# A two-layer hybrid trunk on one core: attention on full 128-row tiles with its transpositions three items behind the scores, the retention output split in parts, and a key projection among the Fourier products

## The reference, cut to what matters

```python
rq, rk, rv, rg, nq, nk, nv, fu, gt = split(h @ w_in)              # for latent and context tokens
y_ret = ((groupnorm(retention(rq, rk, rv)) * gw + gb) * silu(rg)) @ ret_w_out
# neighbourhood attention: 8 heads of 64, 4 rows x 64 columns of latent tokens, 16 columns each, all context keys
s = concat([q @ k_window.T * 64**-0.5 + bias, q @ k_ctx.T * 64**-0.5])
y_na  = (softmax(s) @ v) @ na_w_out
y_fou = fft2(fu).real @ fou_w_out
y = (sigmoid(g_ret) * y_ret + sigmoid(g_na) * y_na + sigmoid(g_fou) * y_fou) @ w_o
```

## Time and profile before

| what | value |
|---|---|
| median of 3 runs | 2544.29 us (2541.22 to 2547.0) |
| profiled execution's own time | 2541.49 us |
| its span, first to last instruction | 2539.7 us |
| mean granted TensorE clock, as a share of full | 0.978 |
| PE busy | 2432.4 us (96% of the span) |
| PE weight loads | 2106.9 us (83%) |
| DVE busy | 1592.9 us (63%) |
| ACT busy | 941.9 us (37%) |
| POOL busy | 131.1 us (5%) |
| DMA | 400.62 MB, mean 158 GB/s |

### The profile page before, as it was taken

One profiled execution on the slowest core, in us unless ns is written; L12 is line 12 of the kernel. 1 busy time (PEld: TensorE's weight loads), 2 busy tenths in 40 slices (PEclk: granted clock), 3 DMA queues, 4 the chain that ended last, 5 costly groups with the idle time before them and its releaser, 6 DMA issues.

```text
span 2539.7 us, 33647 instructions
## 1 busy us (share of the span) xinstructions
PE 2432.4 (96%) x13554; PEld 2106.9 (83%) x13554; DVE 1592.9 (63%) x2098; ACT 941.9 (37%) x1373; POOL 131.1 (5%) x163
## 2 busy tenths in 40 slices
PE   6999999999999999979999999999999998996998
PEld 6988988988876788868889888889888885995996
DVE  5566658755555455486666686666786644665655
ACT  2522345433124322344224554224454213443343
POOL 2000001001000000020000010000020001001000
PEclk8999999999999999989999999999999998997999
DMA  8545665551312334445456565456565232674763
GB/s 269 154 162 167 192 194 177 169 182 34 107 41 70 125 121 136 136 144 168 159 173 192 181 209 167 153 178 192 181 183 177 92 116 81 200 244 136 229 200 124
DMA packets 476815, 400.62 MB, mean 158 GB/s; under 512 B 36341, under 2 KB 428789, under 8 KB 476405
## 3 DMA queue, kind: packets, MB, share of 16 engines
q1 hardware_dynamic: 464992, 391.18, 49.3%
q10 hardware_dynamic: 11668, 7.30, 1.0%
HBM read 397.25 MB, written 1.17 MB: 157 GB/s over the span
## 4 chain that ended last, share of the span: by engine, by line
PE 87%; DVE 7%; ACT 2%; issue 2%; DMA 1%; SPq 0%; POOL 0%; POOLq 0%; ACTq 0%; DVEq 0%
PE ps L1315 26%; PE ps L1317 25%; PE ps L1316 25%; DVE wl L835 2%; PE ps L1579 2%; PE ps L1570 1%; PE ps L1591 1%; PE ps L1513 1%; ACT wh L504 1%; PE ps L1340 1%; ACT tB L522 1%; DVE st L893 1%; PE ps L1672 1%; PE ps L1347 1%; PE ps L1371 1%
## 5 line engine op out<-in xcount | busy, mean ns | idle before, releaser
L835 DVE TENSOR_TENSOR wl<-raw,wh 128x1024 fp32r<-128x1024 f32 x576 | 701.0, 1221 | 665.3 <-ACT wh L504 663.9
L504 ACT ACTIVATE wh<-raw 128x1024 fp32r<-128x1024 f32 x576 | 609.7, 1059 | 1278.8 <-PE ps L1317 1246.3
L1315 PE MATMUL ps<-hh,wh 128*128 128x256 f32 (+1 forms) x2736 | 895.1, 327 | 32.0 <-DVE hl L926 19.8
L1316 PE MATMUL ps<-hl,wh 128*128 128x256 f32 (+1 forms) x2736 | 887.5, 324 | 0.0
L1317 PE MATMUL ps<-hh,wl 128*128 128x256 f32 (+1 forms) x2736 | 887.4, 324 | 0.0
L1315 PEld LDWEIGHTS ps<-hh,wh 128*128 128x128 f32 x2736 | 523.8, 191 | 77.7 <-DVE hl L926 20.9
L1316 PEld LDWEIGHTS ps<-hl,wh 128*128 128x128 f32 x2736 | 523.8, 191 | 41.5 <-issue 1.0
L1317 PEld LDWEIGHTS ps<-hh,wl 128*128 128x128 f32 x2736 | 523.5, 191 | 40.9
L850 DVE SCALAR_TENSOR_TENSOR acc<-araw,c,acc 128x1024 f32<-128x1024 f32 x210 | 258.3, 1278 | 41.1 <-DMA araw<-in_ada_w 39.6
L1315 PE MATMUL ps<-wh,stage_h_f 128*128 128x512 f32 x616 | 240.7, 391 | 2.0 <-DVE stage_l_f L979 2.0
L1316 PE MATMUL ps<-wl,stage_h_f 128*128 128x512 f32 x616 | 239.8, 389 | 0.0
(11 more groups left out here) (158 smaller groups left out, 2360.5 us busy)
## 6 DMA issues: line engine op xcount, KB each, us to landing
raw<-in_ffa_w SPq DMA_DIRECT2D x204, 512.0 KB, 4.0
raw<-in_ffb_w SPq DMA_DIRECT2D x168, 512.0 KB, 3.8
raw<-in_mix_w_in SPq DMA_DIRECT2D x148, 512.0 KB, 4.1
araw<-in_ada_w SPq DMA_DIRECT2D x136, 512.0 KB, 5.1
raw<-in_mix_w_o SPq DMA_DIRECT2D x24, 512.0 KB, 4.3
raw<-in_ret_w_out SPq DMA_DIRECT2D x16, 512.0 KB, 4.5
raw<-in_na_fou_w_out SPq DMA_DIRECT2D x16, 512.0 KB, 3.8
raw<-in_ada_w SPq DMA_DIRECT2D x8, 512.0 KB, 5.4
```

The lines of the kernel that those rows point to most:

```text
L504: A.activation(wh[:, s, :], raw[:, s, :], ACT.Copy).then_inc(w_rounded, 1)
L835: V.tensor_tensor(wl[:, s, :], raw[:, s, :], f(wh[:, s, :]), ALU.subtract).then_inc(w_split, 1)
L1315: T.matmul(out, a[0], b[0], start=start, stop=False)
L1316: T.matmul(out, a[0], b[1], start=False, stop=False)
```

## The change

Scores and values use the whole array. Queries go to `nq`, a slot of 128 partitions for each head in which the other head's 64 rows are zero; values go to `nv` with 128 columns for each head, of which the other head's 64 are zero. POOL writes the zeros ahead of attention. ACT, no longer DVE, copies the queries out of PSUM, in two or four pieces a unit, and copies each tile of values in two pieces. Both heads of a pair add up in one bank. Items are ordered (pair, stream, block, head of the pair), so in layer 0 four items of 512 keys and four of 256 alternate.

DVE no longer builds `jd`; it multiplies `prob` by the reciprocal in place (512 or 256 columns). PE's `turned` is a plain `T.transpose` against `ident`, and the flip is in the order in which ACT's copy writes `probT`. `prob` has four buffers, and the rounds are scores(t), turned(t-3), values(t-4).

The bias has four buffers; ACT's queue issues the loads of four heads, SP's those of the other four, earlier than before. The first gate unit of `merge` goes to bank 7 and stands in PE's list right after turned of round len(items). Retention's output is rounded in three parts and its rest taken in three: the first four of eight 128-feature blocks in round len(items), the others four rounds on, after the last values; PE waits for each part at the row that needs it. The first key unit of `na_in` stands after f_one(1) of the Fourier products, and retention's second score product waits for two tiles only.

```diff
-        in0 = [0, RET[0] + 12]
+        in0 = [0, RET[0] + 8]
-        n_items = [[(h, s, q) for h in range(NH) for s in ... for q in range(LT)]
+        n_items = [[(2 * pr + a, s, q) for pr in range(NH // 2) for s in ... for q in range(LT) for a in range(2)]
+        def q_slot(h):
+            return 4 * (h % 2) + h // 2
 # SP
-                for h in range(2, NH):
-                    sp.wait_ge(n_max, n0[l] + len(n_items[l]) // NH * (h - 1))
+                for h in range(4, NH):
+                    sp.wait_ge(n_max, n0[l] + len(n_items[l]) // 4 * (h // 2 - 2) + 3 + h % 2)
                     load_bias(sp, l, h)
 # ACT
-                        if t >= 3:
-                            act.wait_ge(n_turn, b + t - 2)
+                        if t >= 4:
+                            act.wait_ge(n_turn, b + t - 3)
...
-                    if 2 <= t < len(items) + 2:
-                        v = t - 2
+                    if 3 <= t < len(items) + 3:
+                        v = t - 3
...
-                        A.copy(probT[:, v % 2, 0:n], ps[:, 2 + v % 2, 0:n]).then_inc(n_turnc, 1)
+                        o, y = (a.rearrange("p (a c) -> p a c", c=GRID_W) for a in (probT[...], ps[...]))
+                        A.copy(o[:, :, ::-1] if items[v][1] == 0 else o, y).then_inc(n_turnc, 1)
+                    if t == len(items):
+                        act.wait_ge(n_score, b + len(items))
+                        A.copy(oh[:, 0:4, 0:N], rgz[:, 0:4, 0:N]).then_inc(o_hi, 1)
+                    if t == len(items) + 4:
+                        act.wait_ge(n_out, b + len(items))
+                        for p in (4, 6):
+                            A.copy(oh[:, p:p + 2, 0:N], rgz[:, p:p + 2, 0:N]).then_inc(o_hi, 1)
...
-                for h in range(2):
+                for h in range(4):
                     load_bias(act, l, h)
                 for j in range(8):
                     rounded(u + 4 + j)
+                    if j >= 4:
+                        act.wait_ge(unit_done, u + j + 1)
+                        ... A.activation(nq ..., ACT.Copy, scale=DH ** -0.5), two pieces, four where N > SEQ
 # DVE
-                    V.tensor_scalar(jd[:, t % 3], flip[:] if items[t][1] == 0 else ident[:], nmax[:, t % 3, 3:4], None,
-                                    ALU.mult).then_inc(n_jd, 1)
+                    w = prob[:, t % 4, 0:key_n(items[t])]
+                    V.tensor_scalar(w, w, nmax[:, t % 3, 3:4], None, ALU.mult).then_inc(n_norm, 1)
+                def low(p, n):
+                    dve.wait_ge(o_hi, 3 * l + max(p // 2, 1))
+                    V.tensor_tensor(ol[:, p:p + n, 0:N], rgz[:, p:p + n, 0:N], f(oh[:, p:p + n, 0:N]), ALU.subtract).then_inc(o_lo, 1)
+                    if t == len(items):
+                        low(0, 4)
+                    if t == len(items) + 4:
+                        dve.wait_ge(n_out, b + len(items))
+                        low(4, 2)
+                        low(6, 2)
 # PE
-                pe.wait_ge(rv_copied, NT * (l + 1))
-                scores(1)
+                pe.wait_ge(rv_copied, NT * l + 2)
+                scores(1)
+                pe.wait_ge(rv_copied, NT * (l + 1))
...
-                        ins = T.matmul(ps[:, 2 + t % 2, w], prob[:, t % 3, w], jd[:, t % 3], start=True, stop=True)
+                        ins = T.transpose(ps[:, 2 + t % 2, w], prob[:, t % 4, w], ident[:])
...
-                for t in range(len(items) + 3):
+                pe.wait_ge(nq_zero, 2 * l + 2)
+                pe.wait_ge(nv_zero, l + 1)
+                for t in range(len(items) + 4):
                     if t < len(items):
                         scores(t)
-                    if 2 <= t < len(items) + 2:
-                        turned(t - 2)
-                    if t >= 3:
-                        values(t - 3)
+                    if 3 <= t < len(items) + 3:
+                        turned(t - 3)
+                    if t == len(items):
+                        form_a(AT["merge", l], 7, (hh, hl), mid(l))
+                    if t >= 4:
+                        values(t - 4)
...
+                    if t == 1:
+                        pe.wait_ge(in_copied, c0 + 3 + RET[l] + 1)
+                        form_a(AT["na_in", l], 0, src, TOK)
...
-                    if mm == 0:
-                        pe.wait_ge(o_lo, 2 * (l + 1))
-                    form_a(v + 1, 1, (oh, ol), N)
+                    form_a(v + 1, 1, (oh, ol), N, src_at={0: (o_lo, 3 * l + 1), 4: (o_lo, 3 * l + 2), 6: (o_lo, 3 * l + 3)} if mm == 0 else {})
```

More of the change, by code:

```diff
@@ L205, in trunk @@
             fl = sb("fl", [P, FG, TOK], F32R, scope=mix)
+            with Scope() as s:
+                nq = sb("nq", [P, NH, TOK], scope=s)
             ah = sb("ah", [P, FG, TOK], F32R, scope=mix)
@@ L626, in attention @@
                 per = len(items) // NH
-                for t in range(len(items) + 4):
+                for t in range(len(items) + 5):
                     if t < len(items):
@@ L804, in _ @@
                     G.tensor_tensor(rve[:, t % 4], rve[:, t % 4], nhalf, ALU.pow).then_inc(r_rstd, 1)
+                pool.wait_ge(r_fin, r0[l] + len(r_items[l]))
+                for a in range(2):
+                    p0 = DH - DH * a
+                    G.memset(nq[p0:p0 + DH, 4 * a:4 * a + 4, 0:mid(l)], 0.0).then_inc(nq_zero, 1)
+                pool.wait_ge(nq_zero, 2 * l + 2)
+                pool.wait_ge(f_two, f0[l] + len(f_items[l]))
+                for a in range(2):
+                    ins = G.memset(nv[:, :, a::2, DH - DH * a:P - DH * a], 0.0)
+                ins.then_inc(nv_zero, 1)
                 for h in range(NH):
-                    pool.wait_ge(bias_in[h % 2], 16 * ROWS * (l * NH // 2 + h // 2 + 1))
-                    b = bias[:, h % 2].rearrange("p q (r c) -> p (q r) c", c=GRID_W)
+                    pool.wait_ge(bias_in[h % 4], 16 * ROWS * (l * NH // 4 + h // 4 + 1))
+                    b = bias[:, h % 4].rearrange("p q (r c) -> p (q r) c", c=GRID_W)
                     G.tensor_tensor(b, b, wmask[:].unsqueeze(1).broadcast_to([P, LT * ROWS, GRID_W]), ALU.add)\
@@ L1135, in maximum @@
                             dve.wait_ge(bias_masked, NH * l + h + 1)
-                        link(V.tensor_tensor(y[:, 0:SEQ], y[:, 0:SEQ], bias[:, h % 2, q], ALU.add))
+                        link(V.tensor_tensor(y[:, 0:SEQ], y[:, 0:SEQ], bias[:, h % 4, q], ALU.add))
                     link(V.tensor_reduce(nmax[:, t % 3, 0:1], y[:, 0:key_n(items[t])], AXX, ALU.max))
                     V.tensor_scalar(nmax[:, t % 3, 1:2], nmax[:, t % 3, 0:1], -1.0, None, ALU.mult).then_inc(n_max, 1)
-                for t in range(len(items) + 4):
+                def low(p, n):
+                    dve.wait_ge(o_hi, 3 * l + max(p // 2, 1))
+                    V.tensor_tensor(ol[:, p:p + n, 0:N], rgz[:, p:p + n, 0:N], f(oh[:, p:p + n, 0:N]), ALU.subtract).then_inc(o_lo, 1)
+                for t in range(len(items) + 5):
                     if t < len(items):
@@ L1320, in ready, with form_a @@
                 pe.wait_ge(w_split, u + 1)
-            def form_a(u, bank, src, n, kts=KD, row=0, last=True, n0=0):
+            def form_a(u, bank, src, n, kts=KD, row=0, last=True, n0=0, src_at={}):
                 s = u % RING
@@ L1736, in constants @@
     k = {"k_ident": np.eye(P, dtype=f32)}
-    flip = np.zeros((P, P), f32)
-    for r in range(P // GRID_W):
-        for c in range(GRID_W):
-            flip[r * GRID_W + GRID_W - 1 - c, r * GRID_W + c] = 1
-    k["k_flip"] = flip
     swap = np.zeros((P, P), f32)
```

97 lines of the change are left out of this document (46 added, 51 removed).

## The result

The changed kernel takes 2504.88 us, the median of four runs (2501.32 to 2511.34), where the kernel before took 2544.39 (2541.22 to 2547.0): a ratio of 0.985 (95% interval 0.9829 to 0.9872), 39.5 us less. The forecast was 2502. The profiled run took 2506.22 with a span of 2504.3, 35.3 less than the profiled run before.

What follows compares the result with a forecast made beforehand. PE bounds the kernel (87% of the chain), in attention a ring of waits would; savings of 24.0 + 17.5 + 3.6 less 1, 1, 0.2 and 1 make 41.9 us, taking 2541.5 to 2499.6, with 2.8 for the median 2502; range 2490 to 2519.

Steps and rivals of the forecast that it cites:

- The sum: Whole kernel: attention 24.0 + 17.5, Fourier 3.6, less 1, 1, 0.2 and 1, saves 41.9 us.
- the stretches behind them: Stages after attention: give nothing back, since merge and wo are filled by PE alone.
- Full tiles and transpositions: PE's 512-key attention item: scores 0.85, four transpositions 0.44, values 0.87, together 2.16 us instead of 3.16.
- DVE's product: Attention, DVE's 512-column product in place: 0.48 us, between 0.37 and 0.69.
- The ring: Attention: waits from scores through exponential, ACT's copy and values to later scores set 2.31 us per 512-key item, 1.30 per 256-key.
- Stages: Attention's first product to first oh product: 76.5 us in layer 0, 55.0 in layer 1, saving 24.0 and 17.5.
- The 2.5 us charged in layer 0 for a half clock: Start of layer 0's attention: a 5 us stretch at half clock, costing 2.5 us (0 to 6).
- Late rounds: Attention's last rounds: exponentials stay 3.81 us apart in layer 0 and 4.75 in layer 1.
- Fourier: Fourier loop, both layers: the key unit fills PE's waits of 1.94 and 1.67 us, saving 3.6, at least 2.5.
- Retention: Retention's earlier second score product: saves nothing; if the clock halves, some 1 us lost (0 to 3, both layers).
- Bias loads: ACT's 16 bias DMAs, 10.6 us, ahead of rounding unit 4 of na_in: cost 1 us (0 to 3) in layer 1.
- Rival C: Attention: the clock stays at half throughout, PE's 512-key item takes 4.3 us, kernel 2565 us, slower than before; chance 6%.

Runs made afterwards that it cites:

- copy_first: Changed kernel with ACT's copy of item t-3's transposed tile put ahead of the exponential of item t: 2487.2 us.
- bias_spread: Changed kernel with ACT's 16 bias loads issued four at a time behind the first four weight roundings instead of all ahead of them: 2500.2 us.
- key_back: Changed kernel with the first key unit put back behind the Fourier products: 2505.8 us.
- ret_back: Changed kernel with retention's second score product waiting again for all four copies of the values: 2505.7 us.
- half_tiles: Changed kernel with scores back on 64-row tiles and values on 64-column tiles, transpositions and order kept: 2520.8 us.
- scores_half: Changed kernel with only the scores back on 64-row tiles, values on full tiles: 2521.0 us.

## Why the prediction was right, point by point

The sum was 41.9 for a measured 35.3 (profiled) or 39.5 (medians); its terms were right in kind, and their errors have both signs, so the total is better than its parts: the attention stages saved 45.0 for a forecast 41.5, and the stretches behind them, put at nothing, took 6.9 more in the profiled run.

- **Full tiles and transpositions, 0.85, 0.44, 0.87 and 2.16 an item.** Measured 0.86, 0.44, 0.89 and 2.19, undisturbed only with the copy first. The prediction credited the transpositions with 0.65; 0.45 is theirs and 0.2 the switch's. DVE's product, estimated at 0.48, took 0.487.
- **The ring.** Right, by copy_first. 2.31 an item was forecast; in layer 1 at full clock scores stood 2.19 to 2.56 apart with one step of 3.27, 2.46 in the mean. In layer 0 long and short items can't be told apart as they were priced, since a round holds the scores of one item and the values of the fourth before it: steps are 1.53 to 2.56 in either kind. A head pair, four items of each kind, took 15.98 (762.12 to 778.10) for a forecast of 4 x 2.31 + 4 x 1.30 + 1.2 = 15.6; the sum is right, the division into 2.31 and 1.30 is not shown.
- **Stages.** 76.5 and 55.0 forecast, 75.3 and 52.75 measured. The 2.5 us charged in layer 0 for a half clock did not come, though PE waited 1.88 there; in layer 1 the clock was half for some 3.2 us at the start and as long in the last rounds (0.87 of 12.4 us, 0.93 of 23.3). That layer 0 was spared is luck of this execution: with the same attention code it took 75.3 in bias_spread, but 77.0 in key_back and 78.7 in ret_back, at clocks of 1.00, 0.96 and 0.93.
- **Late rounds** unchanged at 3.81 and 4.75: right.
- **Fourier, 3.6.** 2.2 to 2.4 in layer 0 and 2.1 in layer 1 where it stands, a little more than forecast. No wait stands before the first `f_two`. In layer 1 the bias loads took it back and more: the stretch from Fourier to attention grew by 1.6.
- **Retention, nothing, 1 for the clock.** The loss was 1.8 in the profiled run; ten other profiled runs with the same order don't have it.
- **Bias loads, 1 (0 to 3).** Mis-sized: 3.7 in the profile (72.4 to 68.7) and 4.7 by bias_spread's median. I saw the 10.6 us on ACT's queue but set them against DVE's pace behind the burst, not against the backlog: the first split came 11.2 us late, and DVE had too little slack to make it up before PE's value units.
- **Rival C, the half clock (6%).** It did not come, but the reason given against it, that the full clock had held through half-used tiles in the earlier trace rows, was weak. half_tiles and scores_half show that half tiles between transpositions can keep the clock down, for some 40 us in the profiled runs. Had the change kept half tiles, it would have given some 16 of its 39.5 us back.
The Trainium skill, "TensorE: Matmul & The Clock Gate", Part 4, says that transpositions don't count as PE-busy for the clock gate; the traces bear on it from both sides, since with full tiles the clock stayed full with them (1.00 in the windows from 739 to 814) and with half tiles they went with the longer half-clock stretch (0.57 to 770 us, against 0.71 to 751 with products). No run isolates it.

## What to carry to other kernels

When one engine's work in a pipelined loop is cut, look first at the order in which each helping engine serves the loop's items: a short operation that finishes an old item should stand ahead of the long one that starts a new item. Here that order, two blocks exchanged, was worth 17.7 us after the rewrite had brought 39.5. And queue time for loads counts even where the loads are early: put them between the engine's own operations rather than ahead of them.

## What the runs showed of the hardware

- Zero-padded full tiles are faster than half tiles twice over: no switch (0.19 us less at the scores, 0.14 to 0.2 at the transpositions or products, and 0.13 at the values) and, in the profiled runs, the higher clock (1.00 against 0.56 in layer 0's first 32 us).
- DVE can be held up by POOL. DVE's scaling L1156 takes 0.487 us; the one that starts with POOL's bias mask L840 took 1.57, and ended 0.29 after POOL. DVE's and POOL's timelines of the changed kernel (copy_first's longest is 1.41):

```profile
2099.50 1.57 DVE L1156 TENSOR_SCALAR prob<-prob,nms 128x512 f32<-128x512 f32 x1
```
```profile
2099.51 1.27 POOL L840 TENSOR_TENSOR bias<-bias,wmask 128x512 f32<-128x512 f32 x1 [6.61 <-DMA bias<-rpb_table]
```

No run takes the mask away, but the traces agree: over the changed kernel and the twelve others 58 scalings took longer than usual, and each of them met a bias mask and ended 0.14 to 0.29 us after it; none of the 549 that met no mask was longer. The longest step between scores at full clock, 3.27 us from 2101.73, follows it.
